# A quarter of the out-projection ahead of the product with V in an attention step, and an early remainder one step later

## The chip, the cores and the metric

The kernel runs on one core of one Trainium2 chip. The metric is the device time of one execution in microseconds (us); lower is better. The time before is the median of 3 runs.

## The reference, cut to what matters

One layer of a hybrid model on 1024 tokens with 16 meta tokens ahead of them, width 1024: three mixers (a state-space one, a gated linear recurrence, differential attention), an out-projection, then a mixture of 16 experts, and a last norm. The change lies where attention and the out-projection are interleaved:

```python
# diff_attention: 4 heads, 2 logit maps (c) of 64 wide keys each, values 128 wide
s = jnp.einsum('bqhcd,bkhcd->bhcqk', q[:, qs:qe], k[:, :qe]) * scale
p = jax.nn.softmax(jnp.where(causal, s, MASK_VALUE), axis=-1)
a = p[:, :, 0] - lam * p[:, :, 1]
outs.append(jnp.einsum('bhqk,bkhv->bqhv', a, v[:, :qe]))
...
o = rms_norm(o, subln_g) * (1.0 - lam_init)
...
mixed = jnp.concatenate([y_ssm, y_rec, y_att], axis=-1)
h = h + mixed @ w_out[layer]
h = h + hier_moe(rms_norm(h, norm_ffn_g[layer]), ...)
```

Of the 1024 rows of `w_out`, the first 512 belong to `y_ssm` and `y_rec`, which are finished before attention (the early half), and the last 512 to `y_att` (the late half).

## The kernel before, in words

Every engine has its own list of instructions, written out by hand, and runs it in order; engines meet only at semaphores (`wait_ge`). The projection, the two recurrent mixers, attention, the router and the experts follow one another.

Attention takes the tokens in 8 tiles of 128 queries, the last tile (7) first, because `tile_of(p)` is 7 - p. With 4 heads that makes 32 jobs, job n being head n % 4 of tile `tile_of(n // 4)`. A job of tile i sees 16 + 128(i + 1) keys, so jobs get shorter as the stage goes on. All engines run through the same steps n = 0 to 40. In step n:

- TensorE computes the two logit maps of job n (`pe_logits`, L1780 and L1785). They have one set of PSUM banks, so this waits for the exponentials of job n - 1.
- VectorE takes the two row maxima (`dve_maximum`, L1605), ScalarE the two exponentials (L1661), and VectorE, at the head of its step n + 1, joins the two maps into one (`dve_combine`, L1616 to L1619). This join waits for the evacuation of the product with V of job n - 2, since both use the same buffers.
- TensorE then works off a list called `ring`, whose entries alternate between two PSUM banks; an entry waits until the entry two before it has been evacuated (`ring_free`). Kinds: "t", the joined probabilities of job n - 1 turned in groups of up to four 128-blocks (L1804, and L1802 for the meta keys), which ScalarE copies out (L1722, L1724); "o", the product of job n - 2 with V (L1810, L1811), which ScalarE scales out (L1730); "m", the four heads of a finished tile turned (L1815), which ScalarE copies as the rounded part of the late half (L1738); "x", "r" and "s" (L1819, L1825, L1829), transposes and router logits of a finished tile. In a step the order is t, o, s, m, x, r.
- At the end of a step from n = 6 on, TensorE does a quarter of an out-projection (`pe_out_quarter`): tile part p has its quarters 0, 1, 2, 3 in steps 4p + 6 to 4p + 9. Quarters 0 and 1 multiply the early half, 2 and 3 the late half. A quarter is 12 matmuls of 128x512: inputs and weights are each split in a rounded part and a remainder, with three products for each of 4 blocks.

The out-projection has one pair of PSUM banks, 2 and 5. So quarter 0 of part p waits until VectorE has added the sums of part p - 1 to the residual stream (`dve_residual`, L1633, semaphore `h1_ready`), which VectorE does in the same step 4p + 6, behind that step's two maxima and behind the means for the norm of the attention output (`dve_means`, L1625, L1626). Quarter 0 also waits for the remainder of the early half (`dve_early_mix`, L1698), quarter 2 for that of the late half (`dve_late_mix`, L1704, done by VectorE at step 4p + 8 behind the join). The early remainder is taken from the rounded copy that ScalarE makes last in its step 4p + 4 (`act_early_mix`, L1691). GpSimd computes the norm of the attention output between `dve_means` and "m".

Of the kernel before, what the change touches and what calls it, by code (L numbers as in the profile page):

```python
# [27 lines left out]
NT = X // P  # L28
# [82 lines left out]
def build(nc, a, out):  # L111
    ctx = ExitStack()
    with ctx:
# [1375 lines left out]
        def step_of(kind, n):  # L1489

            return n + {"t": 1, "o": 2}[kind] if kind in "to" else 4 * n + {"m": 7, "x": 13 - 2 * (n == NT - 1), "r": 14 - 2 * (n == NT - 1), "s": 15 - 3 * (n == NT - 1)}[kind]

        ring = []
# [64 lines left out]
        def dve_lambda(dve, link):  # L1558
            dve.wait_ge(lame_ready, 1)
            link(nc.vector.tensor_tensor(NLAM, LAME[:, 1:2], LAME[:, 0:1], ALU.subtract))  # L1560
            nc.vector.tensor_scalar(NLAM, NLAM, -LAM_INIT, None, ALU.add).then_inc(nlam_ready, 1)
# [14 lines left out]
        def dve_attention(dve, link):  # L1576
            dve_maximum(dve, 0, 0)
            dve_maximum(dve, 0, 1)
            dve_s5_gated(dve, 0)
            dve_lambda(dve, link)  # L1580
            dve.wait_ge(nlam_ready, 1)
            for n in range(NSTEP):
                if 1 <= n <= NJOB:
                    dve_combine(dve, link, n - 1)
                if n >= 8 and n % 4 == 0 and (n - 8) // 4 < NT:
                    dve_late_mix(dve, (n - 8) // 4)
                if 0 < n < NJOB:
                    dve_maximum(dve, n, 0)
                    dve_maximum(dve, n, 1)
                if n == 1:  # L1590
                    dve_s5_gated(dve, 1)
                if n >= 4 and n % 4 == 0 and (n - 4) // 4 < NT:
                    dve_early_mix(dve, (n - 4) // 4)
                if n >= 6 and n % 4 == 2 and (n - 6) // 4 < NT:
                    dve_means(dve, link, (n - 6) // 4)
                if 10 <= n < 10 + NJOB and n % 4 == 2:
                    dve_residual(dve, (n - 10) // 4)
                if 11 <= n < 11 + NJOB and n % 4 == 3:
                    dve_normed(dve, (n - 11) // 4)

        def dve_maximum(dve, n, c):
            dve.wait_ge(qk_done, 2 * n + c + 1)
            if n >= 2:
                dve.wait_ge(exp_done, 2 * (n - 2) + c + 1)
            nc.vector.tensor_reduce(NMX[:, 2 * (n % 2) + c:2 * (n % 2) + c + 1], logits(c)[:, KEY0:KEY0 + keys_of(n)], AX.X, ALU.max,  # L1605
                                    negate=True).then_inc(max_ready, 1)
# [75 lines left out]
        def early_halves(p, i):  # L1682
            t = tile_of(p)
            return MIX[i][:, 0:2, P * t:P * t + P], slice(2 * i, 2 * i + 2)
# [9 lines left out]
        def dve_early_mix(dve, p):  # L1694
            dve.wait_ge(xhi_ready, X_DONE + p + 1)
            for i in range(2):
                x, ks = early_halves(p, i)
                ins = nc.vector.tensor_tensor(MLOE[:, ks], x, MHIE[:, ks].bitcast(F32), ALU.subtract)  # L1698
            ins.then_inc(xlo_ready, 1)
# [46 lines left out]
        def pe_attention(pe):  # L1746
            pe.wait_ge(o_copied, 4)
            pe.wait_ge(prd_ready, 1)
            nc.tensor.matmul(LAMS, con[0:64, C_ONES:C_ONES + P], PRD[0:64], start=True, stop=True, skip_group_check=True).then_inc(lam_sum, 1)
            pe_logits(pe, 0)  # L1750
            pe.wait_ge(glu_gate, 4)
            pe_turn_outputs(pe, 1)
            pe.wait_ge(hgrn_done, 4)
            for n in range(4, 6):
                pe_glu(pe, n)
            r = 0
            for n in range(NSTEP):
                if n == 1:
                    pe.wait_ge(lame_ready, 1)
                if 0 < n < NJOB:  # L1760
                    pe_logits(pe, n)
                if n == 1:
                    for m in range(6, 8):
                        pe_glu(pe, m)
                    pe.wait_ge(s5_done, 4)
                while r < len(ring) and step_of(*ring[r][:2]) <= n:
                    pe_ring(pe, r)
                    r += 1
                if n >= 6 and (n - 6) // 4 < NT:
                    pe_out_quarter(pe, (n - 6) // 4, (n - 6) % 4)  # L1770

        def pe_logits(pe, n):
            i, h = tile_of(n // 4), n % 4
# [16 lines left out]
        def pe_ring(pe, r):  # L1790
            kind, n, g = ring[r]
            if r >= 2:
                pe.wait_ge(ring_free, r - 1)
                if ring[r - 2][0] == "m":
                    pe.wait_ge(xlo_ready, late_split(ring[r - 2][1]))
            b = slot(r)
            if kind == "t":
                pe.wait_ge(a_ready, n + 1)
                A = PR_[n % 2][:, 0]
                for j, v in enumerate(g):  # L1800
                    if v == "meta":
                        mm = nc.tensor.transpose(b[0:META, P * j:P * j + P], A[:, 0:META], ident)  # L1802
                    else:
                        mm = nc.tensor.transpose(b[:, P * j:P * j + P], A[:, META + P * v:META + P * v + P], ident)  # L1804
            elif kind == "o":
                h = n % 4
                pe.wait_ge(ring_free, at_ready[n])
                vc = slice(512 + P * h, 512 + P * h + P)
                for k in range(tile_of(n // 4) + 1):
                    nc.tensor.matmul(b[:, 0:P], AT[n % 2][:, k], V[:, 1 + k, vc], start=(k == 0), stop=False)  # L1810
                mm = nc.tensor.matmul(b[:, 0:P], AT[n % 2][0:META, 8], V[0:META, 0, vc], start=False, stop=True)  # L1811
            elif kind == "m":
                pe.wait_ge(oa_ready, n + 1)
                for j, h in enumerate(g):
                    mm = nc.tensor.transpose(b[:, P * j:P * j + P], OA[:, n % 2, P * h:P * h + P], ident)  # L1815
            elif kind == "x":
                pe.wait_ge(h1_ready, n + 1)
                for j, k in enumerate(g):
                    mm = nc.tensor.transpose(b[:, P * j:P * j + P], H1R[:, n % 2, P * k:P * k + P], ident)  # L1819
            elif kind == "r":  # L1820
                pe.wait_ge(ring_free, xt_at[n])
                pe.wait_ge(pool_filled, 5)
                for k in range(KD):
                    j = k % 4
                    mm = nc.tensor.matmul(b[32 * j:32 * j + 32, 0:P], WRT[:, k], XT2[:, n % 2, k], start=(k < 4), stop=(k >= 4))  # L1825
            else:
                pe.wait_ge(ring_free, part_at[n])
                pe.wait_ge(pool_filled, 6)
                mm = nc.tensor.matmul(b[:, 0:20], RPART, FOLD[:, 0:20], start=True, stop=True)  # L1829
            mm.then_inc(ring_ready, 1)  # L1830

        def pe_out_quarter(pe, p, q):

            t, h, late = tile_of(p), q % 2, q // 2
            if q == 0:
                pe.wait_ge(late_loaded, 32)
                if p:
                    pe.wait_ge(h1_ready, p)
                if EARLY_SPLIT:
                    pe.wait_ge(xlo_ready, early_split(p))  # L1840
                    pe.wait_ge(wlo_ready, wo_split(3))
            if q == 2:
                pe.wait_ge(ring_free, mix_at[p])
                pe.wait_ge(xlo_ready, late_split(p))
                pe.wait_ge(wlo_ready, wo_split(KD - 1))
            for k in range(4 * late, 4 * late + 4):
                o, wl = ps[:, 2 + 3 * h, :], WOL_T[k][:, 512 * h:512 * h + 512]
                if k < WSPLIT0:
                    nc.tensor.matmul(o, mix(k)[:, P * t:P * t + P], WO[:, k, 512 * h:512 * h + 512], start=(k == 0), stop=False)
                    continue  # L1850
                x, lo = (MHIE[:, k], MLOE[:, k]) if k < 4 else (MHIL[:, k - 4, P * t:P * t + P], MLOL[:, p % 2, k - 4])
                nc.tensor.matmul(o, x, wo_high(k)[:, h], start=(k == 0), stop=False)
                nc.tensor.matmul(o, x, wl, start=False, stop=False)
                mm = nc.tensor.matmul(o, lo, wo_high(k)[:, h], start=False, stop=(k == KD - 1))
            if q == 1:
                mm.then_inc(early_used, 1)
            if q == 3:
                mm.then_inc(out_done, 1)
# [764 lines left out]
```

## Time and profile before

| what | value |
|---|---|
| median of 3 runs | 1205.26 us (1199.12 to 1207.63) |
| the profiled execution | 1204.86 us, span of its instructions 1203.0 us, mean granted TensorE clock 0.958 |
| TensorE matmul busy | 1073.4 us (89% of the span) |
| VectorE, ScalarE, GpSimd busy | 845.6, 639.0, 482.3 us |

The span runs from the first to the last instruction of the profiled execution; the time lies 1.9 us above it. All times inside the kernel are counted from the start of the span. A share of busy time is an average over stages. Attention proper lies between about 420 and 688 us, and steps 6 to 37, which have a quarter of the out-projection, between about 470 and 683 us.

### The profile page before, as it was taken

Reading aid. Unit: us, or ns where it says so; the run is one execution under the profiler, and the core shown is the slowest. Engines: PE = TensorE matmul, PEld = TensorE weight load, DVE = VectorE, ACT = ScalarE, POOL = GpSimd, SP = SyncE. Lnnn points to the kernel's source line nnn. Section 1 sums busy time; section 2 is a strip of 40 time slices with the busy share of each in tenths; the row PEclk is TensorE's granted clock in tenths of the full one; section 3 lists DMA queues with packets and bytes.
Section 4 is the critical chain, followed back from the end, with each engine's and each line's share of the span. In section 5 each row is a group of like instructions: output and inputs, shape, how many; then the busy total and the mean of one; then the engine's idle time right before and its main releaser. Section 6 shows DMA issues by size and latency. Waiting matters only on the chain. (4 is left out here: it accounts for less than half of the span.)

```text
span 1203.0 us, 22049 instructions
## 1 busy us (share of the span) xinstructions
PE 1073.4 (89%) x7126; PEld 895.8 (74%) x7126; DVE 845.6 (70%) x1234; ACT 639.0 (53%) x1008; POOL 482.3 (40%) x303
## 2 busy tenths in 40 slices
PE   4899989999978988999999738999999999999995
PEld 4898988989967645766667626878777788788873
DVE  4797846564356556555554387888787888889987
ACT  5522111166532355544444226778776788788854
POOL 1131211122000225101121114878775788789960
PEclk9999989999977999999999959999999999999988
DMA  7216334332033720001111684688999878877453
GB/s 264 82 44 75 108 94 126 104 114 71 21 72 73 299 94 1 18 37 53 54 71 70 239 301 160 216 262 311 310 381 370 277 264 279 261 261 217 109 163 158
DMA packets 89495, 194.97 MB, mean 162 GB/s; under 512 B 9265, under 2 KB 32049, under 8 KB 88769
## 3 DMA queue, kind: packets, MB, share of 16 engines
q1 hardware_dynamic: 82800, 169.91, 41.3%
q0 software_dynamic: 6624, 24.12, 8.5%
q8 instruction: 45, 0.74, 0.3%
q14 instruction: 26, 0.20, 0.1%
HBM read 220.60 MB, written 31.51 MB: 210 GB/s over the span
## 5 line engine op out<-in xcount | busy, mean ns | idle before, releaser
L2277 PE MATMUL ps<-split 128*128 128x512 f32 x1728 | 417.6, 398 | 17.8 <-DVE split L2375 10.2
L2277 PEld LDWEIGHTS ps<-split 128*128 128x128 f32 x1728 | 321.6, 190 | 95.6 <-DVE split L2375 15.8
L2323 ACT CAST split<-weights 128x1024 fp32r (+1 forms) x288 | 298.1, 1052 | 103.2 <-PE ps L2277 90.5
L2375 DVE TENSOR_TENSOR split<-weights,split 128x1024 fp32r<-128x1024 f32 x216 | 300.0, 1442 | 46.3 <-ACT split L2323 45.2
L480 PE MATMUL ps<-xsplit,wsplit 128*128 128x384 f32 (+2 forms) x1440 | 243.2, 327 | 2.9 <-POOL wsplit L252 2.9
L2220 POOL TENSOR_TENSOR split<-weights,split 128x1024 fp32r<-128x1024 f32 x72 | 203.2, 2823 | 96.7 <-ACT split L2323 96.0
L480 PEld LDWEIGHTS ps<-xsplit,wsplit 128*128 128x128 f32 x1440 | 229.7, 192 | 4.1 <-POOL wsplit L252 3.3
L252 POOL TENSOR_TENSOR wsplit<-mem,wsplit 128x1024 fp32r<-128x1024 f32 x22 | 57.1, 2594 | 251.2 <-ACT wsplit L335 251.2
L1605 DVE TENSOR_REDUCE sml<-ps 128x1 f32<-128x1040 f32 (+7 forms) x64 | 46.6, 769 | 54.2 <-PE ps L1785 54.2
L1722 ACT COPY mem<-ps 128x512 f32<-128x512 f32 (+3 forms) x48 | 21.5, 481 | 113.3 <-PE ps L1804 75.4
L1548 POOL TENSOR_TENSOR sml<-sml 128x4 f32<-128x4 f32 x8 | 8.1, 1015 | 156.2 <-DVE sml L1626 156.2
L335 ACT CAST wsplit<-mem 128x1024 fp32r<-128x1024 f32 x22 | 23.2, 1052 | 86.6 <-DMA mem<-in_w_in 86.6
L2247 POOL DMA_INDIRECT h_d<-par,sml x22 | 53.0, 2408 | 3.5 <-issue 3.0
L1661 ACT ACTIVATE mem<-ps,sml 128x1040 f32<-128x1040 f32 (+7 forms) x64 | 47.1, 736 | 0.0
L1810 PE MATMUL ps<-mem 128*128 128x128 f32 x288 | 40.2, 286 | 6.8 <-ACT mem L1722 6.8
L1810 PEld LDWEIGHTS ps<-mem 128*128 128x128 f32 x288 | 35.6, 195 | 12.4 <-ACT mem L1722 12.0
L2207 POOL DMA_INDIRECT con<-xn_d,sml x24 | 35.4, 1475 | 19.3 <-POOL sml L2204 19.3
L419 ACT COPY mem<-ps 128x384 f32<-128x384 f32 (+2 forms) x48 | 20.5, 450 | 42.4 <-PE ps L480 34.1
L1785 PE MATMUL ps<-mem 64*128 64x400 f32 (+6 forms) x224 | 42.2, 491 | 0.0
L2401 DVE TENSOR_SCALAR par<-ps,sml 128x512 f32<-128x512 f32 x44 | 30.9, 744 | 7.8 <-DMA h_d<-par,sml 7.8
L2328 ACT CAST split<-ps 128x512 fp32r<-128x512 f32 x48 | 25.7, 589 | 17.7 <-PE ps L2257 17.7
L1026 POOL TENSOR_TENSOR sml<-sml 128x16 f32<-128x16 f32 x2 | 7.6, 3801 | 68.1 <-DVE sml L1231 68.1
(434 smaller groups left out, 1641.4 us busy)
## 6 DMA issues: line engine op xcount, KB each, us to landing
weights<-in_w_down SPq DMA_DIRECT2D x26, 2048.0 KB, 15.8
weights<-in_w_gate SPq DMA_DIRECT2D x50, 1024.0 KB
weights<-in_w_up SPq DMA_DIRECT2D x50, 1024.0 KB
mem<-in_w_in SPq DMA_DIRECT2D x22, 512.0 KB, 4.3
mem<-in_x SPq DMA_DIRECT2D x10, 512.0 KB, 3.8
mem<-in_w_out SPq DMA_DIRECT2D x1, 4096.0 KB, 15.3
h_d<-mem SPq DMA_DIRECT2D x8, 512.0 KB, 2.6
xn_d<-mem SPq DMA_DIRECT2D x8, 512.0 KB, 2.6
```

What stands on the lines that cost most here:

```text
L252: nc.gpsimd.tensor_tensor(WLO[i], RAW[i], WHI[i].bitcast(F32), ALU.subtract).then_inc(wlo_ready, 1)
L480: mm = nc.tensor.matmul(ps[:, n % 6, 0:hi - lo], w[slot_of(h)][:, k % 4, P * m:P * m + P], x[:, k, lo:hi], start=(k == 0 and p_ == 0), sto ...
L1605: nc.vector.tensor_reduce(NMX[:, 2 * (n % 2) + c:2 * (n % 2) + c + 1], logits(c)[:, KEY0:KEY0 + keys_of(n)], AX.X, ALU.max, negate=True).t ...
L1661: f(PR_[n % 2][:, c, 0:nk], logits(c)[:, KEY0:KEY0 + nk], ACT.Exp, bias=NMX[:, o:o + 1], accum_out=SUM[:, o:o + 1]).then_inc(exp_done, 1)
L1785: mm = nc.tensor.matmul(logits(c)[:, s:e], AQ[R, h, P * i:P * i + P], AK[R, h, s - lo:e - lo], start=(e != hi), stop=True, skip_group_chec ...
L1810: nc.tensor.matmul(b[:, 0:P], AT[n % 2][:, k], V[:, 1 + k, vc], start=(k == 0), stop=False)
L2207: pool.indirect_dma_start(XG[:, par], None, xn_d, bass.IndirectOffsetOnAxis(ap=ixc[:, par:par + 1], axis=0)).then_inc(xg_loaded[par], 16)
L2220: nc.gpsimd.tensor_tensor(WL[place % RING], raw(kind, k, q), WH[place % RING].bitcast(F32), ALU.subtract).then_inc(wl_pool, 1)
L2247: pool.indirect_dma_start(h1_d, bass.IndirectOffsetOnAxis(ap=sixc[:, 1 - par:2 - par], axis=0), YE, None, compute_op=ALU.add).then_inc(ye_ ...
L2277: mm = nc.tensor.matmul(ps[:, bank + h, :], x, w[place % RING][:, 512 * h:512 * h + 512], start=(k == 0 and p_ == 0), stop=(k == n - 1 and ...
L2323: nc.scalar.copy(WH[place % RING], raw(kind, k, q)).then_inc(wh_ready, 1)
L2375: nc.vector.tensor_tensor(WL[place % RING], raw(kind, k, q), WH[place % RING].bitcast(F32), ALU.subtract).then_inc(wl_dve, 1)
```

## The change

In each step TensorE first does only the "t" entries of the ring, then the quarter of the out-projection, then the rest of the ring. The order within the ring, and with it the use of the two banks, stays. VectorE takes the early remainder in step 4p + 5 instead of step 4p + 4, at the same place behind the two maxima. No instruction is added or removed.

```diff
                 if n == 1:
                     dve_s5_gated(dve, 1)
-                if n >= 4 and n % 4 == 0 and (n - 4) // 4 < NT:
-                    dve_early_mix(dve, (n - 4) // 4)
+                if n >= 5 and n % 4 == 1 and (n - 5) // 4 < NT:
+                    dve_early_mix(dve, (n - 5) // 4)
...
-                while r < len(ring) and step_of(*ring[r][:2]) <= n:
+                while r < len(ring) and ring[r][0] == "t" and step_of(*ring[r][:2]) <= n:
                     pe_ring(pe, r)
                     r += 1
                 if n >= 6 and (n - 6) // 4 < NT:
                     pe_out_quarter(pe, (n - 6) // 4, (n - 6) % 4)
+                while r < len(ring) and step_of(*ring[r][:2]) <= n:
+                    pe_ring(pe, r)
+                    r += 1
```

## Rows read from the trace of the kernel before

**Rows 1.** Busy time by stretch, steps 7 to 37 (x: instructions; PEclk: granted clock).

```profile
475.00:689.00 214.00, 198.03 (x1215) 145.63 (x1214) 106.83 (x192) 92.83 (x269) 38.07 (x46) 1.00 0.20 72
```

**Rows 2.** TensorE's waits, 474 to 689 us (total us, times, longest).

```profile
PE ps L1810 <- ACT mem L1722: 6.0, 14, 0.6
PE ps L1852 <- issue: 4.6, 5, 1.1
PE ps L1815 <- ACT mem L1744: 1.8, 3, 0.7
```

**Rows 3.** Timeline of step 14, which has quarter 0 of part 2.

```profile
537.76 1.59 DVE L1605 TENSOR_REDUCE sml<-ps 128x1 f32<-128x656 f32 x2 [3.50 <-PE ps L1785]
...
538.26 0.27 PE L1802 MATMUL ps<-con,mem 128*16 128x128 f32 x1
...
538.99 1.38 PE L1810 MATMUL ps<-mem 128*128 128x128 f32 x10 [0.46 <-ACT mem L1722]
...
540.05 1.29 DVE L1633 TENSOR_TENSOR mem<-ps,mem 128x512 f32<-128x512 f32 x2
...
540.71 0.64 PE L1825 MATMUL ps<-mem 128*32 128x128 f32 x16
...
541.44 0.47 PE L1852 MATMUL ps<-wo_higher,mix_early 128*128 128x512 f32 x1
```

**Rows 4.** Timeline of TensorE, quarter 0 of parts 1 and 6 (steps 10, 30).

```profile
505.33 0.27 PE L1802 MATMUL ps<-con,mem 128*16 128x128 f32 x1
...
508.67 0.47 PE L1852 MATMUL ps<-wo_higher,mix_early 128*128 128x512 f32 x1 [0.70 <-issue]
...
648.84 0.27 PE L1802 MATMUL ps<-con,mem 128*16 128x128 f32 x1
...
649.68 0.64 PE L1825 MATMUL ps<-mem 128*32 128x128 f32 x16
...
651.39 0.47 PE L1852 MATMUL ps<-wo_higher,mix_early 128*128 128x512 f32 x1 [1.07 <-issue]
```

**Rows 5.** Timeline of step 15, from logits to join and late remainder.

```profile
544.30 0.28 PE L1780 MATMUL ps<-con 128*128 128x128 bf16 x2
...
545.83 0.76 PE L1804 MATMUL ps<-con,mem 128*128 128x128 f32 x5
...
548.47 0.48 PE L1811 MATMUL ps<-mem 16*128 16x128 f32 x2
...
548.99 0.37 ACT L1730 ACTIVATE mem<-ps,sml 128x128 f32<-128x128 f32 x1
...
549.91 0.90 DVE L1619 SCALAR_TENSOR_TENSOR mem<-mem,sml 128x656 f32<-128x656 f32 x1
550.10 0.59 ACT L1738 CAST mix_late<-ps 128x512 fp32r<-128x512 f32 x1 [0.61 <-PE ps L1815]
...
550.74 0.68 DVE L1704 TENSOR_TENSOR par_split<-ps,mix_late 128x512 fp32r<-128x512 f32 x1
```

**Rows 6.** Timeline of steps 4 and 5 across engines.

```profile
458.21 0.37 ACT L1730 ACTIVATE mem<-ps,sml 128x128 f32<-128x128 f32 x1 [0.41 <-PE ps L1811]
...
460.15 2.40 DVE L1698 TENSOR_TENSOR mix_early_lower<-mem,mix_early 128x256 fp32r<-128x256 f32 x2 [4.35 <-ACT mix_early L1691]
...
464.23 1.63 PE L1804 MATMUL ps<-con,mem 128*128 128x128 f32 x7 [4.11 <-DVE mem L1619]
```

**Rows 7.** TensorE in chosen stretches: busy, granted clock, DMA share, GB/s.

```profile
94.70:96.70 2.00, 0.02 (x1) 1.00 0.00 0
96.70:100.00 3.30, 3.30 (x23) 1.00 0.78 113
434.20:436.70 2.50, 0.00 (x0) 1.00 0.82 189
437.00:440.30 3.30, 3.30 (x12) 0.51 0.77 309
464.40:467.60 3.20, 3.20 (x16) 0.50 0.00 0
```

## The prediction

> **What bounds the kernel now.** I began with busy time by stretch, because the change touches one stage only: from step 7 to step 37 TensorE is busy for 198.0 of 214 us at the full clock, VectorE for 107, ScalarE for 93 [rows 1]. TensorE is the engine that the stage runs on. So an edit can win at most the 16 us that it stands idle there, and whatever idle time an edit adds is paid in full, unless it takes the place of other idle time. Next, TensorE's waits: 6.0 us in 14 waits of 0.2 to 0.6 us before the product with V, for ScalarE's copy of the turned probabilities (ring slots); 4.6 us in five waits before a quarter of the out-projection; 1.8 us before "m" [rows 2]. The five waits before a quarter are put down to "issue", so I looked at the timeline for what ended just ahead of them. It is the residual addition: in step 14 VectorE ends it at 541.34, and quarter 0 starts at 541.44, with all of TensorE's other work of the step, up to the end of "r" at 541.35, in front of it [rows 3]. That is the row on which this prediction rests: quarter 0 already starts at the moment that the residual allows, and what stands before it on TensorE is the cover.
>
> **Part 1: the product with V goes behind the quarter.** I go through the four kinds of step.
>
> Quarter 0 (steps 10, 14, ... 30, six times with full steps, and 34). It needs the addition of the sums of the part before, which VectorE does in the same step, behind the two maxima, which need this step's logits. Nothing in the change moves that. In step 14 the transposes end at 538.53 (538.26 + 0.27) and the residual at 541.34; TensorE now has nothing to do in between and waits 2.9 us, where before it waited 0.46 us for a copy and nothing for the residual [rows 3]. What it did there, the product with V and "r", 538.99 to 541.35 or 2.4 us, comes behind the quarter and is added to the step. In step 10 the same reading gives 508.67 - 505.60 = 3.1 us of wait, of which 0.7 were idle before and about 0.35 were a copy's wait, so 2.0 us more; in step 30, the shortest, 651.39 - 649.11 = 2.3 us of wait, 1.07 idle before, so 1.2 us more [rows 4]. Mean of the three: 1.9 us, six times, 11.2 us. Step 34 has no logits, but VectorE must do its means before the residual, and these need the last product, which now comes late; I take 1.2 us there too, the smallest of the above. Sum: +12.4 us.
>
> Quarters 1, 2, 3: here the gain is. A quarter of 2.9 us covers ScalarE's copies. Three of the 14 waits of [rows 2] lie in steps with quarter 0, where the new wait swallows them, so 11/14 of 6.0 us go: -4.7 us. The wait for "m" was behind evacuations that ScalarE could not start in time, and goes as well: -1.8 us [rows 2].
>
> What is late next. VectorE's join of job n waits for the evacuation of job n - 2's product, and the transposes of step n + 1 wait for the join. In step 15 the product ends at 548.95, the evacuation at 549.36, the join at 550.81: 1.86 us [rows 5]. Before, a quarter and the next logits lay over it; now only the logits do, 1.53 us from 544.30 to 545.83 in that tile. With 0.1 us of hand-over that leaves a wait of 0.4 us. Where "x", "r" or "m" (at least four transposes, some 0.6 us by the five of 0.76) stand behind the product they fill most of it, so the waits are in the steps after 6 to 12, where "x" and "r" do not exist yet, and after 16, 20, 24 and 28: eleven times 0.45 us, +5.0 us. I take a little over 0.4, because the bare wait grows as the logits get short and the fixed part of the chain stays.
>
> Quarter 2 also needs the late remainder, which VectorE takes behind the join: 0.68 us [rows 5]. The transposes run beside it; the five of tile 4 take 0.76 us, and the last tiles have two to four. Three times about 0.5 us for the short tiles. For the last part no transposes are left: after "m" come ScalarE's copy (0.59), the remainder (0.68) and three hand-overs of 0.1, bare, because quarter 1 now stands ahead of "m" and no longer covers them: 1.5 us. Together +3.0 us. The first expert's weights are requested after that copy, so they follow the shift; the request comes at most the same 1.5 us later against the end of the stage, which I cost at nothing, since the router's work stands between the two.
>
> **Part 2: the early remainder a step later.** In step 4 VectorE waited 4.35 us for ScalarE's rounded copy and then took until 462.55 for the remainder, two instructions in 2.40 us; only then did the join of that step begin, and TensorE waited 4.11 us for it [rows 6]. The evacuation that the join needed had ended at 458.58 (458.21 + 0.37). With the remainder out of the way the join would be ready some 1.7 us later (the 1.45 us of [rows 5] from evacuation to join, and more for the wider tile), at 460.3, against logits that end at 460.12: a wait of 0.2 us, 3.9 us saved. If the join is slowed as the remainder was (two instructions of 256 columns in 2.40 us, against 0.68 us for one of 512 columns in [rows 5]; some 1.6 us), it is 2.3. I take 3.4. After that wait the granted clock was 0.50, the lower of the two levels, for 3.2 us [rows 7]; the time this cost was partly hidden by copies, and I take half of 1.6 us: another 0.8. Sum: -4.2 us. The later seven postponements cost nothing: quarter 0 comes a step after the remainder, and in step 4p + 5 VectorE has slack.
>
> **The clock.** In steps 7 to 37 it is granted in full [rows 1]. The new waits of 2.3 to 3.1 us are of another size than those there. A stand of 2.00 us before 96.7 was followed by full clock; one of 2.5 us before 436.7 by 0.51 for 3.3 us [rows 7]. So waits of the new length lie at the edge or past it. At half clock 3.3 us of matmuls do the work of 1.65. With four of seven waits followed by a fall, 1.5 us lost at each (part of the lower clock can lie in the wait itself), +6 us; none is 0, all seven 11.5.
>
> The Trainium skill, page "TensorE: Matmul & The Clock Gate", section "HAM oscillation — how this bites in real kernels", warns of kernels in which every burst of matmuls begins cold after a wait, but its rule of thumb lets pauses as short as these pass. By it the sum would be that of the second case below. Row 434.20 to 436.70 shows a fall after a shorter stand than the page asks for, so I go by the row.
>
> **Sum.** 12.4 - 4.7 - 1.8 + 5.0 + 3.0 - 4.2 = +9.7 us without the clock, +15.7 us with it. The profiled execution, 1204.86 us, becomes 1220.6; it lies 0.4 us under the median, which changes nothing. Behind attention the work is a chain that starts from its end (router, then experts), so I pass the shift on one to one.
>
> **Rivals.**
> - The clock holds: the seven waits are there and no fall follows. For it: TensorE is busy at full rate on both sides of each wait, unlike around 434. Against: the row of 2.5 us. +9.7 us, 1214.5 us.
> - The worst of both: every wait is followed by a fall, and the join of step 4 is slowed. +9.7 + 11.5 + 1.6 = 22.8, about 1228 us. It decides by how the waits lie.
> - Faster: the covers work and the wait for the residual does not appear, because VectorE ends the addition by the end of the transposes. Then -4.7 - 1.8 + 5.0 + 3.0 - 4.2 = -2.7 us, and, should ScalarE's evacuations also keep up so that the join isn't late, -10.7 us: 1194 to 1202 us. It would need the residual 2.3 to 2.9 us earlier than in every one of the steps read; nothing moves it.
> - The change does not act: what TensorE waits for is moved within the stage, but the experts' weights or the HBM set the later end. For it: the later stage has transfers on its chain. Against: these are requested from the end of attention on. Within 5 us of 1205.
>
> **Chances.** Forecast with some falls 0.50; clock holds 0.25; worst 0.13; no net effect 0.08; faster 0.04. The range reaches over the first three and their unknown costs: 1210 to 1230 us. One per cent, 12 us, is about what a measurement of this kernel can tell. The case with the clock held lies below it (1214.5 against 1217.3), as does some of the forecast's own low side: slower 0.67, within 1% 0.29, faster 0.04.
>
> **What the profile after would show.** Before the first matmul of quarter 0 in steps 10 to 34 seven waits of 2.3 to 3.1 us, ended by L1633; no waits of L1810 on L1722 in steps with a quarter; short waits of L1804 for L1619 and of L1852 in quarter 2; the wait of 4.11 us in step 4 shrunk; PEclk below 1.00 behind some of the seven. The stage from 475 to 689 us would be busy for the same 198 us at full clock, and longer by the sum. I would be wrong if the residual addition turned out to end before the transposes, or if the gain of step 4 were larger than its wait.

## The result and the profile after

The changed kernel takes 1214.57 us (median of 6 runs, 1212.8 to 1221.96) against 1199.01 us for the kernel before (6 runs): 1.0132 times, with a 95% interval of 1.0097 to 1.0168. It is slower, by 15.6 us. A second set of runs gave a ratio of 1.0090 (1.0059 to 1.0120), about 11 us, so the loss is between about 7 and 20 us. The profiled execution took 1221.96 us, a long one. Attention ends at 701.95 in it, against 688.36 before, although it had entered its second step (its logits, 434.06 against 436.70) 2.6 us earlier. So attention itself is 16.2 us longer. The rest of the program, from there to the end of the span, took 518.1 us against 514.6; the change touches nothing in it, and the difference is within what runs of one kernel differ by.

The busy time of the stretch of [rows 1], up to its later end (the columns are as there):

```profile
475.00:702.00 227.00, 197.69 (x1175) 150.37 (x1173) 90.36 (x185) 91.13 (x261) 29.68 (x37) 0.95 0.18 65
```

Much the same matmuls fill a longer stretch, and the granted clock, 1.00 before, is 0.95. (Some 40 records fewer are counted, because the changed kernel is further on in its work at 475 us: step 7 begins at 469.31 us in it and at 477.88 us before.) TensorE's waits from 475 us on, against [rows 2] (the change moved the lines by three, so L1855 is L1852 of before, L1807 is L1804, L1813 is L1810):

```profile
PE ps L1855 <- issue: 18.3, 8, 2.9
PE ps L1807 <- DVE mem L1619: 5.2, 11, 0.8
...
PE ps L1855 <- ACT mix_late L1738: 1.4, 1, 1.4
```

L1813 is not in this list: from step 6 on no product waits for a copy any more. In its place stand 18.3 us before a quarter. The timeline of step 14, against [rows 3]:

```profile
532.19 1.59 DVE L1605 TENSOR_REDUCE sml<-ps 128x1 f32<-128x656 f32 x2 [0.70 <-PE ps L1788]
...
532.69 0.27 PE L1805 MATMUL ps<-con,mem 128*16 128x128 f32 x1
...
534.48 1.29 DVE L1633 TENSOR_TENSOR mem<-ps,mem 128x512 f32<-128x512 f32 x2
...
535.87 0.66 PE L1855 MATMUL ps<-wo_higher,mix_early 128*128 128x512 f32 x1 [2.91 <-issue]
...
540.29 1.28 PE L1813 MATMUL ps<-mem 128*128 128x128 f32 x10
...
541.91 0.64 PE L1828 MATMUL ps<-mem 128*32 128x128 f32 x16
```

The transposes end at 532.96, the residual addition at 535.77, and quarter 0 starts at 535.87, after 2.91 us. Product and "r" come behind it. Of the first matmul look at the duration too: 0.66 us, where the same line took 0.47 us in [rows 3]. The lower clock begins 0.13 us after its start and holds for most of the quarter, which the next view shows. Columns are the stretch, its length, TensorE's busy time, granted clock, DMA share and GB/s, as in [rows 7]:

```profile
533.00:535.80 2.80, 0.00 (x0) 1.00 0.47 176
536.20:539.40 3.20, 3.20 (x9) 0.50 0.41 164
627.60:630.00 2.40, 0.00 (x0) 1.00 0.55 162
630.10:633.40 3.30, 3.30 (x16) 1.00 0.46 184
```

After a stand of 2.9 us the clock is at the lower level; after one of 2.4 us at 630 it is not. Lower-clock stretches begin at 498.5, 536.0, 570.1, 600.9 and 655.5 us, each within one of the seven waits or less than 1 us behind it, and one at 669.1, behind waits of 0.4 and 0.7 us. Together they last 23.9 us. The early remainder, against [rows 6]: in step 4 the join's wait has shrunk from 4.11 us.

```profile
455.27 0.37 ACT L1730 ACTIVATE mem<-ps,sml 128x128 f32<-128x128 f32 x1 [0.41 <-PE ps L1814]
...
457.51 0.96 PE L1807 MATMUL ps<-con,mem 128*128 128x128 f32 x7 [0.33 <-DVE mem L1619]
```

### The profile page after: what moved, and what is told of

Read it like the earlier page. It is cut to its first block, busy times and chain, and to the rows that moved or that the text cites. A ratio compares the mean times of both kernels' runs of the same rounds, so it can differ in the third digit from the quotient of the medians.

```text
span 1220.2 us, 22049 instructions
## 1 busy us (share of the span) xinstructions
PE 1076.3 (88%) x7126; PEld 903.2 (74%) x7126; DVE 830.7 (68%) x1234; ACT 641.2 (53%) x1008; POOL 475.2 (39%) x303
## 4 chain that ended last, share of the span: by engine, by line
PE 61%; DVE 15%; issue 6%; ACT 6%; DMA 6%; SPq 4%; POOL 1%; ACTq 0%; DVEq 0%; POOLq 0%
PE ps L2280 25%; PE ps L480 8%; PE ps L1855 3%; DMA weights<-in_w_up 3%; PE ps L1813 3%; PE ps L1856 3%; PE ps L1857 3%; DVE split L2378 2%; SPq L322 2%; PE ps L1807 2%; PE ps L2260 2%; PE ps L1385 1%; PE ps L1788 1%; PE ps L492 1%; ACT split L2326 1%
## 5 line engine op out<-in xcount | busy, mean ns | idle before, releaser
L2280 PE MATMUL ps<-split 128*128 128x512 f32 x1728 | 417.0, 398 | 21.7 <-DVE split L2378 12.7
L2223 POOL TENSOR_TENSOR split<-weights,split 128x1024 fp32r<-128x1024 f32 x72 | 196.7, 2731 | 104.7 <-ACT split L2326 103.9
L1616 DVE RECIPROCAL sml<-sml 128x2 f32<-128x2 f32 x32 | 5.3, 166 | 119.7 <-ACT mem L1730 115.4
L1730 ACT ACTIVATE mem<-ps,sml 128x128 f32<-128x128 f32 x32 | 11.8, 368 | 93.8 <-PE ps L1814 93.7
L1813 PEld LDWEIGHTS ps<-mem 128*128 128x128 f32 x288 | 37.3, 193 | 4.3 <-ACT mem L1722 1.7
L1813 PE MATMUL ps<-mem 128*128 128x128 f32 x288 | 38.0, 277 | 0.9 <-ACT mem L1722 0.9
```

Source lines behind the costliest of these rows:

```text
L2223: nc.gpsimd.tensor_tensor(WL[place % RING], raw(kind, k, q), WH[place % RING].bitcast(F32), ALU.subtract).then_inc(wl_pool, 1)
L2280: mm = nc.tensor.matmul(ps[:, bank + h, :], x, w[place % RING][:, 512 * h:512 * h + 512], start=(k == 0 and p_ == 0), stop=(k == n - 1 and ...
```

## The experiments

Times are medians; a ratio is always to runs of the kernel before on the same chip. "Stage" is the length from the logits of step 2 to the end of the last router logits in the profiled execution: 251.7 us before, 267.9 us changed.

**The early remainder alone.** The order on TensorE is that of before.

```diff
-                if n >= 4 and n % 4 == 0 and (n - 4) // 4 < NT:
-                    dve_early_mix(dve, (n - 4) // 4)
+                if n >= 5 and n % 4 == 1 and (n - 5) // 4 < NT:
+                    dve_early_mix(dve, (n - 5) // 4)
```

> The order of TensorE's ring as before, only the early remainder one step later. My theory: the wait of 4.11 us for the join in step 4 shrinks to about 0.3 us, the fall of the clock behind it does not come, and nothing else moves: 4 to 5 us faster than before. Rival (the 4.11 us are only moved, because the exponentials or the copies of step 5 are late next): within 1 us of before, and the wait is found again in steps 5 and 6.

Ratio 0.9955 (0.9930 to 0.9980), 5.4 us faster; the stage is 5.2 us shorter. The transposes of steps 5 and 6 on TensorE, which wait for the joins of jobs 4 and 5:

```profile
457.60 0.95 PE L1804 MATMUL ps<-con,mem 128*128 128x128 f32 x7 [0.33 <-DVE mem L1619]
...
463.64 0.95 PE L1804 MATMUL ps<-con,mem 128*128 128x128 f32 x7 [0.20 <-DVE mem L1619]
```

The wait is 0.33 us, and 0.20 us in the next step; the clock did not fall. Of the 5.2 us, 3.6 are idle time and 1.5 busy time that the lower clock had cost. The rival, that the wait is only moved, is out. This half of the change is a gain.

**The quarter alone.** The changed kernel with the two lines above put back.

```diff
-                if n >= 5 and n % 4 == 1 and (n - 5) // 4 < NT:
-                    dve_early_mix(dve, (n - 5) // 4)
+                if n >= 4 and n % 4 == 0 and (n - 4) // 4 < NT:
+                    dve_early_mix(dve, (n - 4) // 4)
```

> The quarter ahead of the product with V, the early remainder where it was (step 4p + 4). My theory: the product now ends last in its step, ScalarE evacuates it and only then makes the rounded early copy (0.7 us), VectorE takes the remainder (0.8 us) ahead of the join, and the next transposes wait some 1.5 us longer than in the changed kernel in each of the seven steps 4p + 5 from 9 on, on top of the 4 us of step 4: about 26 us slower than before, 10 us slower than the changed kernel. Rival (the two edits add up, no more): the changed kernel plus the 4 to 5 us of the first experiment, about 20 us slower than before.

Ratio 1.0271 (1.0201 to 1.0340), 32 us slower, stage 286.6 us. Engines between product and transposes, step 16 to 17 (L1814 is L1811 of before):

```profile
568.34 0.48 PE L1814 MATMUL ps<-mem 16*128 16x128 f32 x2
...
568.86 0.37 ACT L1730 ACTIVATE mem<-ps,sml 128x128 f32<-128x128 f32 x1 [2.27 <-PE ps L1814]
...
569.13 0.70 ACT L1691 CAST mix_early<-mem 128x256 fp32r<-128x256 f32 x2
569.86 0.76 DVE L1698 TENSOR_TENSOR mix_early_lower<-mem,mix_early 128x256 fp32r<-128x256 f32 x2 [4.78 <-ACT mix_early L1691]
...
570.99 0.77 DVE L1619 SCALAR_TENSOR_TENSOR mem<-mem,sml 128x528 f32<-128x528 f32 x1
...
571.90 1.09 PE L1807 MATMUL ps<-con,mem 128*128 128x128 f32 x4 [1.76 <-DVE mem L1619]
```

The chain is as my theory had it: the product ends, ScalarE evacuates and makes the rounded copy, VectorE takes the remainder and only then the join, and the transposes wait 1.76 us. Before, all this lay beside the quarter. The loss is 24 to 41 us by the interval, which holds my 26 us and not quite the rival's 20. In the profile it is larger than I had it because of the clock: beside 3.8 us for the join of job 4 and 1.2 us in each of six later steps, 11.0 us of waits more than in the changed kernel, the lower clock now holds for 37.5 us instead of 23.9. Three of its stretches begin in or right behind waits for a join of 1.76, 1.93 and 2.01 us. The two edits do not add up: the early remainder is worth 5 us alone and 17 to 22 us with the quarter first (1.0271 against 1.0132, or against the 1.0090 of the second set). Whoever puts the quarter first needs the other half of the change.

**Quarter first, except where it is quarter 0.**

```diff
-                while r < len(ring) and ring[r][0] == "t" and step_of(*ring[r][:2]) <= n:
+                while r < len(ring) and (ring[r][0] == "t" or n % 4 == 2) and step_of(*ring[r][:2]) <= n:
```

> As the changed kernel, but in the steps with a quarter 0 the whole ring comes first, as before. My theory (the waits for the residual and the falls of the clock behind them are the loss): the seven waits of 2.2 to 2.9 us fall back to 1 us or less, the clock stays full from 475 us on, and the kernel is 1 to 5 us faster than before; the waits for the join stay near 5 us. Rival (the loss is the late joins and remainders that come with any product at the end of a step): at least half of the 15.6 us stays, 8 us or more slower than before.

Ratio 0.9955 (0.9923 to 0.9987), 5.2 us faster than before, stage 246.7 us, and the clock is full from 441 us to the end of the stage. TensorE's waits:

```profile
PE ps L1807 <- DVE mem L1619: 4.4, 8, 0.8
PE ps L1855 <- issue: 4.0, 6, 1.0
...
PE ps L1813 <- ACT mem L1722: 1.4, 3, 0.6
```

The waits for joins stay at 4.4 us, while the loss is gone. So late joins are a price of the change, and quarter 0 with what follows from it is the loss.

**Residual added a step earlier.** VectorE adds as soon as quarter 3 is done, which with the quarter first is early in the step.

```diff
-                if 10 <= n < 10 + NJOB and n % 4 == 2:
-                    dve_residual(dve, (n - 10) // 4)
+                if 9 <= n < 9 + NJOB and n % 4 == 1:
+                    dve_residual(dve, (n - 9) // 4)
```

> As the changed kernel, but VectorE adds the residual at the end of its step 4p + 9, as soon as quarter 3 is done, instead of in step 4p + 10 behind the maxima. My theory: no wait before quarter 0 is left, the clock stays full, and what remains are the gains: copies hidden (4.9 us before), step 4 (4 to 5 us), against some 8 us of waits for joins and remainders: 8 to 11 us faster than before. Rival (VectorE then waits for quarter 3 and adds for 1.3 us ahead of its join, and the transposes of the next step wait for that instead): each of seven steps keeps 1 us or more, and the kernel is within 3 us of before.

Ratio 0.9890 (0.9849 to 0.9930), 12.6 us faster than before, a little more than my 8 to 11; stage 238.6 us. Steps 13 and 14:

```profile
522.59 1.29 DVE L1633 TENSOR_TENSOR mem<-ps,mem 128x512 f32<-128x512 f32 x2 [1.65 <-PE ps L1857]
...
527.36 0.27 PE L1805 MATMUL ps<-con,mem 128*16 128x128 f32 x1
...
527.39 0.48 PE L1855 MATMUL ps<-wo_higher,mix_early 128*128 128x512 f32 x1
...
530.24 1.28 PE L1813 MATMUL ps<-mem 128*128 128x128 f32 x10
```

The addition ends at 523.88, 3.5 us ahead of quarter 0, which runs into the transposes without a seam. The waits:

```profile
PE ps L1807 <- DVE mem L1619: 5.7, 12, 0.8
...
PE ps L1855 <- ACT mix_late L1738: 1.4, 1, 1.4
```

No wait for the residual; joins 5.7 us. TensorE's list of instructions is here that of the changed kernel, word for word, only VectorE's differs. So the difference of 29.3 us between the two stages is all due to when VectorE adds, and what goes with it is the wait before quarter 0 and the clock: TensorE's idle time in the stage falls from 32.4 to 15.0 us, 17.4 us less, and its busy time from 235.5 to 223.6 us, 11.9 us less for the same matmuls. 11.9 us is also half of 23.9 us, the time at the lower clock. The rival, that VectorE would then be late with its join, holds for small change only: 5.7 us of waits against 5.2.

**The wait filled.** The changed kernel with eight extra matmuls in each of the seven waits; they write to the bank that the next ring entry overwrites.

```diff
+                if n >= 10 and n % 4 == 2 and (n - 6) // 4 < NT:
+                    pe.wait_ge(ring_free, r - 1)
+                    for _ in range(8):
+                        nc.tensor.matmul(slot(r), wo_high(4)[:, 0, 0:P], wo_high(4)[:, 0], start=True, stop=True)
                 if n >= 6 and (n - 6) // 4 < NT:
                     pe_out_quarter(pe, (n - 6) // 4, (n - 6) % 4)
```

> The changed kernel, with eight further 128x512 matmuls in each step with quarter 0 from step 10 on, written into the bank of the next product with V (which overwrites them) and placed in the wait for the residual; they are extra work and read nothing of this step. Eight take 1.9 us at full clock, less than each of the waits of 2.2 to 2.9 us. My theory (about 12 us of the changed kernel are matmuls at half clock, behind the falls that the waits bring): the residual is ready at the same point, most falls between 475 and 690 us go, the stage gets 8 to 12 us shorter, and the kernel is 4 to 8 us slower than before instead of 15.6. Rival (the waits cost what their length says and the low clock lies mostly beside other waits): within 3 us of the changed kernel, 12 us or more slower than before.

Ratio 1.0060 (1.0030 to 1.0090), 1207.43 us, as forecast; the rival's 12 us or more lies outside. In the same set the changed kernel ran again.

> The changed kernel again, on the chip of the other runs of this set. Every theory: 1.0132 times before, 13 to 19 us slower.

It came to 1.0090 (1.0059 to 1.0120), 1214.89 us, 7 to 14 us slower than before and so mostly under the 13 to 19 us expected. The stages are 258.1 and 269.7 us. TensorE in step 14, filled (L1809 is the last of the transposes, L1772 the filling, L1859 quarter 0), and the busy time of the stage:

```profile
533.25 0.27 PE L1809 MATMUL ps<-con,mem 128*16 128x128 f32 x1
533.98 2.11 PE L1772 MATMUL ps<-wo_higher 128*128 128x512 f32 x8 [0.46 <-ACT mem L1722]
536.43 0.47 PE L1859 MATMUL ps<-wo_higher,mix_early 128*128 128x512 f32 x1 [0.35 <-issue]
```

```profile
475.00:695.00 220.00, 204.57 (x1248) 155.62 (x1248) 92.16 (x187) 93.81 (x265) 31.69 (x39) 1.00 0.19 66
```

Quarter 0 still starts 2.9 us behind the transposes (533.52 to 536.43), as the residual commands, and in the five other steps that have transposes it starts as late behind them as in the changed kernel. But its first matmul takes 0.47 us, and from 475 us on the clock never falls. That is the cost of the clock by itself, with quarter 0 held up as long as it was: 9.8 us against the stage of the profile after, 11.6 us against the repeated one. Over the whole kernel it is less certain: the medians differ by 7.5 us, the ratios by 0.3% or 3.6 us, and the two intervals overlap, so here the profiles carry the size. The repeated run also shows that a fall is not fixed for a wait. In it all seven waits have a fall within them or at most 1.4 us behind them, also the one of 2.44 us, which kept the clock in the profile after:

```profile
629.40:631.70 2.30, 0.00 (x0) 1.00 0.56 153
633.40:636.60 3.20, 3.20 (x11) 0.51 0.13 52
```

**Where to put the quarter first.** Two kernels with the earlier residual. One has the quarter first in steps 4p + 1 throughout and in 4p + 2 and 4p + 3 from 13 to 20; the other everywhere but in steps with quarter 2.

```diff
-                while r < len(ring) and ring[r][0] == "t" and step_of(*ring[r][:2]) <= n:
+                while r < len(ring) and (ring[r][0] == "t" or not (n % 4 == 1 or (12 < n <= 20 and n % 4))) and step_of(*ring[r][:2]) <= n:
```

> As the kernel with the earlier residual, but the quarter comes first only in steps 4p + 1, and in steps 4p + 2 and 4p + 3 from 13 to 20; elsewhere the whole ring is first, as before. My theory (in the other steps a product at the end makes the next join or the late remainder late, by more than the copy's wait that it hides): waits for joins fall from 7.5 to about 3 us, those before quarter 2 vanish, some waits for copies come back (about 2 us), and the kernel is 0 to 4 us faster than with the quarter first everywhere, 1.1 to 1.5% faster than before. Rival (quarter first is worth more than the waits that it hides, because the matmuls on both sides run into each other without a seam): 0 to 4 us slower than with the quarter first everywhere.

Ratio 0.9859 (0.9830 to 0.9888), 1186.84 us, stage 237.2 us.

```profile
PE ps L1813 <- ACT mem L1722: 2.5, 7, 0.5
PE ps L1818 <- ACT mem L1744: 1.8, 3, 0.7
...
PE ps L1807 <- DVE mem L1619: 0.4, 1, 0.4
```

```diff
-                while r < len(ring) and ring[r][0] == "t" and step_of(*ring[r][:2]) <= n:
+                while r < len(ring) and (ring[r][0] == "t" or n % 4 == 0) and step_of(*ring[r][:2]) <= n:
```

> As the kernel with the earlier residual, but in steps with quarter 2 (4p + 8) the whole ring comes first, as before. My theory: the waits for the join at the end of these steps (0.4 to 0.8 us, seven times) and those before quarter 2 (2.5 us in three) go, the copies' waits of steps 8 to 20 come back (0.2 to 0.6 us, four times): 2 to 5 us faster than with the quarter first everywhere, 1.2 to 1.6% faster than before. Rival (the waits for joins move to another step): no difference from the quarter first everywhere.

Ratio 0.9907 (0.9870 to 0.9943), 1190.36 us, stage 238.7 us.

In the first, waits for joins fall to 0.4 us, copies' waits of 2.5 and 1.8 us (L1813 is the product, L1818 "m") come back, and the waits before quarter 2 are gone. Idle time in the stage is 11.8 us against 15.0 with the quarter first everywhere, but busy time is 225.4 against 223.6 us, so that 1.4 us of 3.2 remain. The second waits 12.7 us and is busy 226.0 us: its stage is no shorter than with the quarter first everywhere, and my 2 to 5 us did not come. Half of its 2.4 us of further busy time comes with the order on TensorE, as in the first; the other 1.2 us are the lower clock, which it has for all of 3.4 us at the start of the stage and from 671.2 us to its end. Here the rival of the first kernel had part of the truth: putting the quarter first is worth more than the waits it hides. The intervals of these kernels overlap; all are faster than before, and the first, 1.1 to 1.7% or 13 to 20 us, is the fastest kernel of this study by its median.

## Why the prediction was right, point by point

Forecast +15.7 us, measured +15.6 us by the first medians and about 11 by the second set. That the first agrees to 0.1 us is luck. The forecast 1220.6 us also lies 6 us above the measured 1214.57, because the kernel before came out at 1199.01 in the 6 runs, not at 1205.26. By its time alone the result would fit the rival with the clock held (1214.5 us) as well; what decides between them is the trace and the experiments. The steps:

- **Waits before quarter 0.** Forecast 2.3 to 3.1 us at seven places. Measured 2.76, 2.91, 2.76, 2.59, 2.44, 2.28 and 2.18 us, 17.9 us. Less what was idle in these steps before (4.6 us before the quarter, 1.4 us for copies) that is some 12 us more, against 12.4 forecast. The reading of the rows, that quarter 0 already started when the residual let it, gave the size. The earlier residual shows the cause: with it the waits are gone.
- **Copies.** Forecast -4.7 us and -1.8 us for "m". Measured: no product waits for a copy in a step with a quarter, and "m" waits 0.13 us.
- **Joins and late remainders.** Forecast eleven waits and 5.0 us. The view from 475 us on also has eleven, in 5.2 us, but not the same ones: with one of 0.33 us in step 7, ahead of 475 us, nine of the eleven named steps have a wait, 4.8 us together. Steps 8 and 12 have none; "m" stands behind the product in the steps before them, a cover that I had counted elsewhere and not here. Steps 27, 31 and 32 have 0.8 us that I had not named. For the late remainders, forecast 3.0 us, measured 0.41, 0.68 and 1.44 us, 2.5 us. One of the joins, with the evacuation that it waits for (L1814 is the end of the product):

```profile
521.75 0.48 PE L1814 MATMUL ps<-mem 16*128 16x128 f32 x2
...
522.27 0.37 ACT L1730 ACTIVATE mem<-ps,sml 128x128 f32<-128x128 f32 x1 [2.39 <-PE ps L1814]
...
523.20 0.90 DVE L1619 SCALAR_TENSOR_TENSOR mem<-mem,sml 128x656 f32<-128x656 f32 x1
...
524.25 0.74 PE L1807 MATMUL ps<-con,mem 128*128 128x128 f32 x5 [0.49 <-DVE mem L1619]
```

  Product's end to join's end 1.87 us (522.23 to 524.10), as [rows 5] gave.
- **Step 4.** Forecast 3.4 us of wait saved and 0.8 us of clock, with 3.9 as the upper end. Measured 3.8 us of wait, and 5.4 us in all when the edit runs alone. So the gain is larger than the wait of 4.11 us, which I had named as a sign of being wrong; it was a poor sign, since my own sum had 4.2 us, and the excess is the clock. The join was not slowed as the remainder had been.
- **Sum of the waits.** 12.4 - 4.7 - 1.8 + 5.0 + 3.0 - 3.4 = +10.5 us forecast; TensorE's idle time in the stage rose from 22.0 to 32.4 us, by 10.4.
- **The clock.** This term was mis-sized. I took four falls at 1.5 us, +6 us. Measured: lower clock for 23.9 us, which costs 11.9 us, about what I had put down for all seven; five of seven waits were followed by a fall, the first by one of 6.8 us, and a sixth fall came without a long wait. The filled wait gives 9.8 to 11.6 us. The case "the clock holds" is out. Of "the worst of both" the falls came true in the repeated run, seven of seven, and the slowed join did not.
- **What made up for it** I had not seen. The matmuls of the stage are busy for less time when the quarter stands between the transposes and the product. With full clock from 475 us on, the stage is busy 228.2 us in the old order (early remainder alone) and 223.6 us in the new (residual earlier): 4.6 us. In [rows 3] the product's first line lasts 1.38 us after a wait, in the rows after 1.28 us, and where the quarter meets the transposes they overlap: 527.39 lies 0.24 us before the modelled end of the transposes (527.63). The two stages from 475 us on, the old order first (columns as in [rows 1]):

```profile
475.00:680.50 205.50, 190.43 (x1172) 140.23 (x1170) 101.81 (x185) 89.77 (x260) 31.09 (x37) 1.00 0.21 74
475.00:673.00 198.00, 186.12 (x1176) 143.03 (x1174) 91.28 (x185) 91.41 (x261) 29.57 (x37) 1.00 0.22 75
```

  The other kernels bear it out. With half of the busy time at the lower clock taken off, which is an estimate of the busy time at full clock, the stage is busy 226.2 and 226.5 us in the two kernels with the old order, 223.3 to 223.8 us in the three that have the quarter first in some steps, and 221.8 to 222.7 us in the four with it first throughout (without the filled one). The net change of busy time, 235.5 - 229.7 = +5.8 us, thus splits by the profiles in between into -1.5 (the fall behind step 4), -4.6 (the order) and +11.9 (the falls), where I had +6 - 0.8 = +5.2. The total was right because the error in the falls and the one in the seams between the quarter and its neighbours, a term that I did not have at all, nearly cancel. That too is luck.
- **The rest of the program** passed the shift on, give or take the 3.5 us by which the two executions differ there; over all ten profiles this part takes 512.9 to 518.2 us.

## What to carry to other kernels

Before moving work behind something that waits, look whether it already starts at the very moment that its semaphore comes. If it does, the work ahead of it is its cover and not its delay, and moving it costs its length, less what was idle before, here 1.2 to 2.5 us seven times. Then look at what produces the semaphore: moving that (the addition a step earlier, two lines on VectorE) turned a loss of 1% into a gain of 1% with the same order on TensorE. And count a wait of TensorE of two to three us as its length and the lower clock behind it: here 17.4 us of idle time brought 11.9 us more.

## What the runs showed of the hardware

- Waits of 2.2 to 2.9 us in an otherwise busy TensorE had a fall to the lower clock in them or at most 1.4 us behind them in five of seven cases in one execution of the changed kernel and in seven of seven in another; the same wait of 2.44 us kept the clock in one and lost it in the other. The Trainium skill, page "TensorE: Matmul & The Clock Gate", section "HAM oscillation — how this bites in real kernels", would let such short pauses pass; here the measurement decides, and it says that they often do not. Eight needless matmuls in each wait (1.9 us of 2.9) kept the clock full in all seven.
- Where waits of 0.4 and 0.7 us followed one another the clock also fell once (669.1 us); in the repeated run and with the earlier residual the same two waits had no fall behind them. What made the difference was not tried.
- The order of a chain of small and large matmuls changes its busy time by some 2% at the same clock (228.2 against 223.6 us for the same instructions). The profile models the ends of matmuls, so how the time is split between busy and idle is rough; but the stage itself is 7.9 us shorter, of which waits make up 3.4. Where in TensorE the rest is saved stays open.
